# A weight-splitting kernel: the low part of every other weight unit on GpSimd instead of VectorE

## The chip, the cores and the metric

The kernel runs on 1 core of one Trainium2 chip. The metric is the device time in microseconds (us) of one execution. The program is written in Bass with its own semaphores: five engines (TensorE, VectorE, ScalarE, GpSimd, SyncE) each run a program of their own, and order between engines exists only where one waits for a count that another has raised. Inside an engine the program runs in the order in which it is written. The profile calls TensorE PE (its weight loads PEld), VectorE DVE, ScalarE ACT, GpSimd POOL and SyncE SP.

## The reference, cut to what matters

Two transformer blocks run one after the other on 256 tokens (272 in the first block, which puts 16 meta tokens ahead), each with two layers, width 1024, all in float32. Nearly all of the arithmetic is products with weight matrices:

```python
# first block, for each layer
h = h + mix                                   # layer 0: chunk scan + attention, layer 1: pooling
h = h + einsum('blf,fd->bld', relu(rmsnorm(h) @ w_mlp_up) ** 2, w_mlp_down)      # d_ff 4096
# second block, for each layer
x = x + rms_norm(mix, g)                      # layer 0: short convolution, layer 1: attention
gate, up = split(causal_dwconv(rms_norm(x) @ w_up, w_conv), 2)                   # 2 x 2816 columns
x = x + rms_norm((silu(gate) * up) @ w_down, g)
x = x + rms_norm(sigmoid(rms_norm(x) @ w_gate) * (p_i @ w_proj), g)
```

## The kernel before, in words

Activations lie with their features on the 128 partitions and the tokens along the free axis. Each product of float32 operands is made of three products of the shorter type fp32r: an operand v is split into a high part (v rounded to fp32r) and a low part (v minus the high part), and high x high, high x low and low x high are summed in PSUM (`products`, lines 333 to 342, the matmul is line 340; the variants `products_rows` and `first_products` have theirs on lines 351 and 385).

The weights are cut into 383 **units** of at most 128 x 1024 elements (`weight_units`, lines 19 to 84), numbered in the order in which TensorE uses them. 365 units are 1024 elements wide, 16 are 768 and 2 are 512. A unit passes through four steps:

- SyncE loads unit n into one of 4 buffers RAW (`load_unit`, line 309), after `wl` of unit n - 4, the sign that the low part of the unit that had the buffer is made.
- ScalarE copies it to fp32r into one of 7 buffers WH (`act_split`, line 318). It waits for the load and for `used` of unit n - 7.
- VectorE subtracts: WL = RAW - WH, into one of 7 buffers WL (`dve_split`, line 325), after `wh` of unit n.
- TensorE waits for `wl` of unit n and uses it in, mostly, 24 matmuls of 128 x 128 by 256 tokens.

The order of the steps is written out by hand. `act_split(a, upto)` and `dve_split(v, upto)` make all units below `upto` that are not yet made; the stages call them in between their own work, so that they run some 6 to 7 units ahead of TensorE. In the feed-forward stages of the second block (`vector_ffn`, lines 1859 to 1950) VectorE's loop runs over u = 0 to 24. Each of its steps covers two units of w_up: for m = 0 and 1 one split (of unit n0 + 2u + m + 6, n0 being the stage's first unit) and one FZ (line 1895, PSUM times the root's row RR); then two products YB (line 1877) or two low parts FL (line 1883); then four convolution taps (line 1457, on GB or YB). ScalarE makes the first tap from FZ (line 1826), the high part FH (line 1798) and its splits in the same order. n0 is unit 197 in the first of these stages (ffn0) and unit 307 in the second (ffn1); both are odd. The down product behind it (`tensor_output`, line 1461) reads FH and FL in blocks of 8, 8 and 6 chunks k and takes two units for each block.

A `Signals` object keeps for each event, such as ("wl", n), the semaphore and the count that stand for it. `mark` raises the semaphore of its kind, `also` makes one event stand for another, and a kind of semaphore may belong to one engine only. All programs are run through dry first, so that each wait knows its count.

GpSimd sets two constants (`gpsimd_start`, line 496) and clears five buffers of the first mixer (`gpsimd_mixer`, line 552). After that its program is over.

Of the kernel before, what the change touches and what calls it, by code (L numbers as in the profile page):

```python
# [12 lines left out]
NR = 4  # L13
NH = 7
# [72 lines left out]
def width(unit):  # L87
    return UW if unit[3] is None else len(unit[3]) * len(unit[4])
# [162 lines left out]
def program(nc, xin, pin, gains, cst, wpack, out):  # L251
    f32, f32r, u32 = mybir.dt.float32, mybir.dt.float32r, mybir.dt.uint32
    ALU, ACT, AX = mybir.AluOpType, mybir.ActivationFunctionType, mybir.AxisListType
    units = weight_units()
# [7 lines left out]
    NU = len(units)  # L262
    scratch = nc.dram_tensor("bias_rows", (8, 384), f32)
    ctx = ExitStack()
    with ctx:
        def sb(name, shape, dt=f32, scope=ctx):
            return scope.enter_context(nc.sbuf_tensor(name, shape, dt))

        sig = Signals(lambda kind: ctx.enter_context(nc.semaphore(f"s_{kind}")))
# [6 lines left out]
        RAW = [sb(f"RAW{i}", [128, UW]) for i in range(NR)]  # L276
        WH = [sb(f"WH{i}", [128, UW], f32r) for i in range(NH)]
        WL = [sb(f"WL{i}", [128, UW], f32r) for i in range(NH)]
# [32 lines left out]
        def act_split(a, upto):  # L311
            while a.units < min(NU, upto):
# [4 lines left out]
                    a.wait_ge("used", n - NH)  # L317
                a.e.activation(WH[n % NH][:, 0:w], RAW[n % NR][:, 0:w], ACT.Copy).then_inc(*a.mark("wh", n))  # L318

        def dve_split(v, upto):  # L320
            while v.units < min(NU, upto):
                n, v.units = v.units, v.units + 1
                w = width(units[n])
                v.wait_ge("wh", n)
                v.e.tensor_tensor(WL[n % NH][:, 0:w], RAW[n % NR][:, 0:w], WH[n % NH][:, 0:w].bitcast(f32),  # L325
                                  ALU.subtract).then_inc(*v.mark("wl", n))
# [169 lines left out]
        def gpsimd_start(p):  # L496
            p.e.memset(ONE[:, :], 1.0).then_inc(*p.mark("ones", 0))
            p.e.memset(EPS[:, :], 1e-6).then_inc(*p.mark("ones", 1))
# [53 lines left out]
        def gpsimd_mixer(p):  # L552
            for i, (z, val) in enumerate(((QB[:, :, :], 0.0), (KB[:, :, :], 0.0), (ATT[:, :, :], 0.0), (ATM[:, :, :], 0.0),
                                          (E[:, :, :], 1.0))):
                p.e.memset(z, val).then_inc(*p.mark("zero", i))
            p.wait_ge("zero", 4)
            p.e.memset(E[:, :, 0:1], 0.0).then_inc(*p.mark("zero", 5))
            p.wait_ge("zero", 5)
            p.e.memset(E[:, :, 16:T:64], 0.0).then_inc(*p.mark("zero", 6))
# [394 lines left out]
        def vector_mixer(v):  # L954
# [6 lines left out]
            def divided(key, uu, dst):  # L961
                for m in range(2):
                    h = 2 * uu + m
                    dve_split(v, unit_at[key, h] + NH - 1)
                    v.wait_ge("mix", key, h)
                    v.wait_ge("rk", "m")
                    v.e.tensor_tensor(dst[:, h, :], PS[:, banks.at[key, h], 0:T], R, ALU.mult).then_inc(
                        *v.mark("ev", key, h))
# [50 lines left out]
            def latent(x):  # L1019
                key = ("cq", "ckv")[x]  # L1020
                dve_split(v, unit_at[key, 0] + NH)
                for m in range(2):
                    o = CQ[:, 2 * x + m, :]
                    v.wait_ge("mix", key, m)
                    v.e.tensor_tensor(o, PS[:, banks.at[key, m], 0:T], R, ALU.mult).then_inc(*v.mark("ev", key, m))
                    v.wait_ge("ch", 2 * x + m)
                    v.e.scalar_tensor_tensor(out=CL[:, 2 * x + m, :], in0=o, scalar=g(("qa", "kva")[x], m),
                                             in1=CH[:, 2 * x + m, :].bitcast(f32), op0=ALU.mult,
                                             op1=ALU.subtract).then_inc(*v.mark("cl", 2 * x + m))
# [91 lines left out]
            v.e.tensor_tensor_scan(flat(B), flat(E), flat(LF), 0.0, ALU.mult, ALU.add).then_inc(*v.mark("scan"))  # L1121
            exponents(0)
            dve_split(v, unit_at["hi", 0] + NH)
            attention(0)
            prepare(0)
# [1192 lines left out]
        def gpsimd_program(p):  # L2318
            gpsimd_start(p)
            gpsimd_mixer(p)  # L2320

        def sync_program(s):
            sync_start(s)
            s.e.dma_start(C[:, :], cst[:, 128:NCA]).then_inc(*s.mark_dma("c"))
            for n in range(NR, NU):
                load_unit(s, n)
            for p in range(4):
                s.wait_ge("x2", "end", p)
                s.e.dma_start(out[:, 2 * p:2 * p + 2, :], X[:, 2 * p:2 * p + 2, NM:T]).then_inc(*s.mark_dma("out", p))
            s.wait_ge("out", 3)  # L2330
# [8 lines left out]
        for fill in (tensor_program, scalar_program, vector_program, gpsimd_program, sync_program):  # L2339
            counted(fill)  # L2340
# [16 lines left out]
        @block.gpsimd  # L2357
        def _(e):
            gpsimd_program(Engine("gpsimd", e, sig))
# [69 lines left out]
```

## Time and profile before

| | |
|---|---|
| Median of 3 runs | 1394.87 us (1394.56 to 1399.25) |
| The profiled execution's own time | 1391.52 us |
| Its span, first to last instruction | 1389.5 us |
| Mean granted clock of TensorE | 0.974 of 2.4 GHz |
| TensorE matmuls busy | 1330.0 us, 96% |
| VectorE busy | 918.8 us, 66% |
| ScalarE busy | 725.1 us, 52% |
| GpSimd busy | 4.5 us, 13 instructions |

The busy time of an engine is the time that at least one of its instructions covers. A row of a group gives busy time and the mean duration of one instruction; instructions of one engine overlap by a little in the records, so the distance between two starts is slightly below the duration. The chain that ended last is followed back from the last instruction, at each step to what released it.

### The profile page before, as it was taken

The page shows a single profiled execution, that of the slowest core. Times are in us where ns is not written, and L with a number is a line of the kernel's source. Part 1 is how long each engine was busy: PE and PEld are TensorE (multiplying, and loading weights), DVE is VectorE, ACT ScalarE, POOL GpSimd, SP SyncE. Part 2 cuts the span into 40 slices and gives each one's busy share as a digit, 9 for nine tenths or more (in the row PEclk, how much of TensorE's full clock was granted, in tenths as well). Part 3 has the DMA queues.
Part 4 walks back from the last instruction along what each step waited for, and adds up shares of the span by engine and source line. Part 5 has one row for each costly group of instructions (what it writes and reads, how often), then busy time and mean ns, then how long its engine had stood idle before and what let it go on. Part 6 is the DMA issues. An engine that isn't in the chain of part 4 may idle for free.

```text
span 1389.5 us, 25078 instructions
## 1 busy us (share of the span) xinstructions
PE 1330.0 (96%) x10558; PEld 1288.7 (93%) x10558; DVE 918.8 (66%) x1505; ACT 725.1 (52%) x1219; POOL 4.5 (0%) x13
## 2 busy tenths in 40 slices
PE   5998899999998999999999999999999999999996
PEld 5897679999998999999999999999987799999996
DVE  4687655765446777444875999746564546999654
ACT  5754234665332666334545666646453446666644
POOL 1000000000000000000000000000000000000000
PEclk9999979999999999999999999999898999999997
DMA  6232005555552465654753666663272133666630
GB/s 257 85 122 81 31 3 150 182 180 170 181 170 75 145 200 175 194 183 129 227 180 118 194 187 196 200 200 106 89 246 66 31 109 106 201 193 192 204 121 31
DMA packets 58415, 205.20 MB, mean 148 GB/s; under 512 B 6328, under 2 KB 8640, under 8 KB 58048
## 3 DMA queue, kind: packets, MB, share of 16 engines
q1 hardware_dynamic: 56816, 201.77, 46.0%
q10 hardware_dynamic: 1488, 1.85, 0.5%
q8 instruction: 83, 1.36, 0.4%
q14 instruction: 28, 0.23, 0.1%
HBM read 202.53 MB, written 1.06 MB: 147 GB/s over the span
## 4 chain that ended last, share of the span: by engine, by line
PE 85%; DVE 8%; ACT 5%; issue 1%; DMA 1%; ACTq 0%; DVEq 0%
PE PS L340 65%; PE PS L385 7%; PE PS L351 2%; PE PS L368 2%; PE PS L419 2%; PE PS L2020 1%; PE PS L2019 1%; ACT WH L318 1%; DVE WL L325 1%; PE PS L466 1%; PE PS L652 1%; DMA HB<-bias_rows 1%; DVE Z L1417 1%; PE PS L784 0%; PE PS L690 0%
## 5 line engine op out<-in xcount | busy, mean ns | idle before, releaser
L325 DVE TENSOR_TENSOR WL<-RAW,WH 128x1024 fp32r<-128x1024 f32 (+2 forms) x383 | 460.5, 1207 | 261.5 <-ACT WH L318 261.2
L318 ACT ACTIVATE WH<-RAW 128x1024 fp32r<-128x1024 f32 (+2 forms) x383 | 391.2, 1042 | 251.3 <-PE PS L340 222.0
L340 PE MATMUL PS<-UH,WH 128*128 128x256 f32 (+1 forms) x1624 | 462.9, 285 | 6.9 <-DVE UL L1402 3.0
L340 PE MATMUL PS<-UH,WL 128*128 128x256 f32 (+1 forms) x1624 | 462.6, 285 | 0.0
L340 PE MATMUL PS<-UL,WH 128*128 128x256 f32 (+1 forms) x1624 | 462.4, 285 | 0.0
L340 PEld LDWEIGHTS PS<-UH,WH 128*128 128x128 f32 x1624 | 309.1, 190 | 7.9 <-issue 4.7
L340 PEld LDWEIGHTS PS<-UH,WL 128*128 128x128 f32 x1624 | 309.1, 190 | 0.0
L340 PEld LDWEIGHTS PS<-UL,WH 128*128 128x128 f32 x1624 | 307.5, 189 | 0.0
L340 PE MATMUL PS<-HL,WH 128*128 128x272 f32 (+1 forms) x512 | 145.8, 285 | 0.0
L340 PE MATMUL PS<-HH,WH 128*128 128x272 f32 (+1 forms) x512 | 145.7, 284 | 0.0
L340 PE MATMUL PS<-HH,WL 128*128 128x272 f32 (+1 forms) x512 | 145.4, 284 | 0.0
L340 PE MATMUL PS<-FH,WH 128*128 128x256 f32 x352 | 98.6, 280 | 0.0
L340 PE MATMUL PS<-FL,WH 128*128 128x256 f32 x352 | 98.5, 280 | 0.0
L340 PE MATMUL PS<-FH,WL 128*128 128x256 f32 x352 | 98.5, 280 | 0.0
L340 PEld LDWEIGHTS PS<-HH,WL 128*128 128x128 f32 x512 | 96.6, 189 | 0.0
L340 PEld LDWEIGHTS PS<-HL,WH 128*128 128x128 f32 x512 | 96.3, 188 | 0.0
L340 PEld LDWEIGHTS PS<-HH,WH 128*128 128x128 f32 x512 | 96.1, 188 | 0.0
L385 PE MATMUL PS<-UH,WH 128*128 128x256 f32 (+1 forms) x256 | 73.9, 289 | 0.2
L385 PE MATMUL PS<-UL,WH 128*128 128x256 f32 (+1 forms) x256 | 72.0, 281 | 0.0
L385 PE MATMUL PS<-UH,WL 128*128 128x256 f32 (+1 forms) x256 | 72.0, 281 | 0.0
L340 PEld LDWEIGHTS PS<-FH,WH 128*128 128x128 f32 x352 | 66.2, 188 | 0.0
L340 PEld LDWEIGHTS PS<-FL,WH 128*128 128x128 f32 x352 | 66.2, 188 | 0.0
(346 smaller groups left out, 1976.9 us busy)
## 6 DMA issues: line engine op xcount, KB each, us to landing
RAW<-wpack SPq DMA_DIRECT2D x365, 512.0 KB, 3.6
RAW<-wpack SPq DMA_DIRECT2D x16, 384.0 KB, 3.5
X<-xin SPq DMA_DIRECT2D x1, 1088.0 KB, 5.1
C<-cst SPq DMA_DIRECT2D x1, 1072.0 KB, 10.0
HB<-bias_rows ACTq DMA_DIRECT2D x1, 1024.0 KB, 7.4
out<-X SPq DMA_DIRECT2D x4, 256.0 KB, 2.3
RAW<-wpack SPq DMA_DIRECT2D x2, 256.0 KB, 3.5
PI<-pin ACTq DMA_DIRECT2D x2, 256.0 KB, 3.1
```

The source lines that it names most:

```text
L318: a.e.activation(WH[n % NH][:, 0:w], RAW[n % NR][:, 0:w], ACT.Copy).then_inc(*a.mark("wh", n))
L325: v.e.tensor_tensor(WL[n % NH][:, 0:w], RAW[n % NR][:, 0:w], WH[n % NH][:, 0:w].bitcast(f32), ALU.subtract).then_inc(*v.mark("wl", n))
L340: ins = t.e.matmul(o, part(n, hw, kw, a, b), x(kx), start=first and not i and not p, stop=last and i == len(kcs) - 1 and p == 2)
L351: ins = t.e.matmul(o, x(kx), part(n, hw, kw, 0, w), start=not i and not p, stop=i == len(kcs) - 1 and p == 2)
L368: t.e.matmul(PS[:, b, 0:256], ONER[:, :], ONER[:, :].unsqueeze(1).to_broadcast([128, 2, 128]), start=True, stop=True)
L385: ins = t.e.matmul(PS[:, b, 0:w], part(n, hw, k, 0, 128), x_(k), start=k == 0 and p == 0, stop=k == 7 and p == 2)
L419: return t.e.matmul(o, src[:, m, a:z], ONE[:, 0:1], start=first and m == 0, stop=last and m == 1)
L466: ins = t.e.matmul(PS[:, b, a:z], rooted(st, x, n).to_broadcast([n, 128]), ID[0:n, 0:n], start=True, stop=True)
L652: ins = t.e.matmul(PS[:, b, 0:T], hot, x, start=n == 0 and hh == 0, stop=n == len(terms) - 1 and hh == 3)
L1417: v.e.tensor_tensor(Z[i][:, :, lo:T], src[:, :, lo:T], src[:, :, lo - k:T - k], ALU.add).then_inc(*v.mark("pz", gi, k))
L2019: t.e.matmul(o, c2("anti"), hb, start=True, stop=False)
L2020: ins = t.e.matmul(o, QH[ps_, h, q0:q0 + 128], KH[ps_, h, 0:w], start=False, stop=True)
```

## The change

GpSimd's program gets a third part. For n = 1, 3, 5, ... 381 it waits for `wh` of unit n and makes WL = RAW - WH with the same subtraction, marks an own semaphore `wlp`, and the event ("wl", n) now stands for it. `dve_split` skips the odd units. ScalarE, SyncE and TensorE are unchanged but for the semaphore on which ("wl", n) of an odd n is waited for.

```diff
+        def gpsimd_split(p):
+            for n in range(1, NU, 2):
+                w = width(units[n])
+                p.wait_ge("wh", n)
+                p.e.tensor_tensor(WL[n % NH][:, 0:w], RAW[n % NR][:, 0:w], WH[n % NH][:, 0:w].bitcast(f32),
+                                  ALU.subtract).then_inc(*p.mark("wlp", n))
+                sig.also(("wl", n), ("wlp", n))
+
         def dve_split(v, upto):
             while v.units < min(NU, upto):
                 n, v.units = v.units, v.units + 1
+                if n % 2:
+                    continue
                 w = width(units[n])
                 v.wait_ge("wh", n)
...
         def gpsimd_program(p):
             gpsimd_start(p)
             gpsimd_mixer(p)
+            gpsimd_split(p)
```

## Rows read from the trace of the kernel before

**Rows 1.** The page, part 1: busy time, share of the span, instructions.

```profile
span 1389.5 us, 25078 instructions
...
PE 1330.0 (96%) x10558; PEld 1288.7 (93%) x10558; DVE 918.8 (66%) x1505; ACT 725.1 (52%) x1219; POOL 4.5 (0%) x13
```

**Rows 2.** The chain that ended last: the page's shares by engine, then shares by line.

```profile
PE 85%; DVE 8%; ACT 5%; issue 1%; DMA 1%; ACTq 0%; DVEq 0%
...
by line: PE PS L340 65.5%; PE PS L385 6.8%; PE PS L351 2.1%; PE PS L368 1.7%; PE PS L419 1.5%; PE PS L2020 1.3%; issue 1.3%; PE PS L2019 1.2%; ACT WH L318 1.1%; DVE WL L325 1.1%; PE PS L466 0.9%; PE PS L652 0.6%; DMA HB<-bias_rows 0.5%; DVE
```

**Rows 3.** The page, part 5: the two groups that split the weights.

```profile
L325 DVE TENSOR_TENSOR WL<-RAW,WH 128x1024 fp32r<-128x1024 f32 (+2 forms) x383 | 460.5, 1207 | 261.5 <-ACT WH L318 261.2
L318 ACT ACTIVATE WH<-RAW 128x1024 fp32r<-128x1024 f32 (+2 forms) x383 | 391.2, 1042 | 251.3 <-PE PS L340 222.0
```

**Rows 4.** Waits of PE: line, releaser: us in total, times, longest us.

```profile
PE PS L419 <- DVE ACC L415: 14.5, 3, 10.2
...
PE PS L340 <- DVE WL L325: 2.7, 1, 2.7
```

**Rows 5.** Windows: busy us of PE, PEld, DVE, ACT, POOL; PEclk, DMA share, GB/s.

```profile
475.00:500.00 25.00, 25.00 (x214) 25.00 (x213) 20.67 (x33) 18.86 (x33) 0.00 (x0) 1.00 0.83 252
...
775.00:800.00 25.00, 25.00 (x214) 25.00 (x213) 24.65 (x48) 16.54 (x27) 0.00 (x0) 1.00 0.64 208
```

**Rows 6.** Timeline of DVE in ffn0: start us, us, line, operation, out<-in.

```profile
773.16 0.42 DVE L1895 TENSOR_TENSOR FZ<-PS,RR 128x256 f32<-128x256 f32 x1
...
777.91 0.42 DVE L1895 TENSOR_TENSOR FZ<-PS,RR 128x256 f32<-128x256 f32 x1
778.25 1.22 DVE L325 TENSOR_TENSOR WL<-RAW,WH 128x1024 fp32r<-128x1024 f32 x1
779.38 0.42 DVE L1895 TENSOR_TENSOR FZ<-PS,RR 128x256 f32<-128x256 f32 x1
779.72 0.75 DVE L1877 TENSOR_TENSOR YB<-YB,GB 128x256 f32<-128x256 f32 x2
...
788.78 0.42 DVE L1895 TENSOR_TENSOR FZ<-PS,RR 128x256 f32<-128x256 f32 x1
```

**Rows 7.** The chain in order of time, ffn0 and ffn1: start us, us, what.

```profile
759.14 2.82 PE PS L340 x24
...
762.40 170.60 PE PS L340 x1446
...
1169.02 170.60 PE PS L340 x1446
```

**Rows 8.** Timeline of PE where the down product of ffn0 begins.

```profile
873.01 0.28 PE L340 MATMUL PS<-FH,WH 128*128 128x256 f32 x1
```

**Rows 9.** Timeline of DVE at the end of ffn0's up stage.

```profile
876.58 0.42 DVE L1895 TENSOR_TENSOR FZ<-PS,RR 128x256 f32<-128x256 f32 x1
...
882.82 0.76 DVE L1883 SCALAR_TENSOR_TENSOR FL<-YB,FH 128x256 fp32r<-128x256 f32 x2
885.62 4.63 DVE L325 TENSOR_TENSOR WL<-RAW,WH 128x1024 fp32r<-128x1024 f32 x4 [2.04 <-ACT WH L318]
```

**Rows 10.** POOL: a group by line and form, and its last instruction in the timeline.

```profile
L555 POOL MEMSET ATT<- 128x1024 f32 x1 | 1.0, 951 | 0.0
...
4.98 0.12 POOL L559 MEMSET E<- 128x16 f32 x1
```

**Rows 11.** The page, part 6: DMA issues, KB each, us to landing.

```profile
RAW<-wpack SPq DMA_DIRECT2D x365, 512.0 KB, 3.6
```

**Rows 12.** Timeline of DVE in the first mixer: two operations of one size.

```profile
45.28 1.28 DVE L1105 SCALAR_TENSOR_TENSOR LF<-LF,B 128x1088 f32<-128x1088 f32 x1
...
47.81 0.73 DVE L1112 TENSOR_SCALAR B<-LF 128x1088 f32<-128x1088 f32 x1
```

**Rows 13.** Mixer, 93 to 125 us: the splits' group on DVE, and the chain there.

```profile
L325 DVE TENSOR_TENSOR WL<-RAW,WH 128x1024 fp32r<-128x1024 f32 x5 | 5.8, 1200 | 0.8 <-ACT WH L318 0.8
...
116.50 2.27 DVE WL L325 x2
```

## The prediction

> **What bounds the kernel now.** I read the busy shares first: TensorE is busy for 96% of the span, VectorE for 66%, GpSimd for nothing to speak of [rows 1]. The chain that ended last says the same: 85% of it are matmuls, 8% VectorE, 5% ScalarE, and the splits of line 325 hold only 1.1% of it, 15.3 us [rows 2]. The waits of TensorE agree: for a low part of a weight it waits once, 2.7 us; its longest wait for VectorE is for a sum of squares [rows 4]. So 460.5 us of splits on VectorE [rows 3] lie beside TensorE nearly everywhere, and an emptier VectorE gives little by itself. What counts is whether VectorE stays fast enough. The windows show where that is tight: in the MLP of the first block it is busy for 20.67 of 25 us at its fullest, but in the feed-forward stages of the second block for 24.65 of 25 us, with TensorE full and its granted clock at 1.00 [rows 5].
>
> How tight, the timelines tell. A pair of steps of the loop over u (4 units) takes VectorE 788.78 - 777.91 = 10.87 us, one step 5.43 [rows 6]. TensorE goes from 762.40, where unit (u=2, m=1) begins, to 873.01, where the down product begins, in 110.61 us for 39 units [rows 7, 8]: 2.836 us each, 5.67 for two. VectorE is thus 0.24 us a step faster, and needs it, as it starts late: unit (2,0) was done at 759.14 + 2.82 = 761.96 [rows 7], its FZ begins at 773.16 [rows 6], 11.2 us behind; the last FZ begins at 876.58 [rows 9], 3.6 us behind 873.01. The low parts FL of the last two chunks are made at 883.58 [rows 9]. TensorE wants them four units and four chunks after 873.01: 873.01 + 4 x 2.836 + 12 x 0.118 = 885.8, 2.2 us later. The next weight unit that VectorE splits (885.62 to 886.8 [rows 9]) is wanted at about 888.6 (four full units and two of 6/8 the length), 1.8 us later. So the stage can bear about **2 us** more of VectorE's time; beyond that TensorE waits one for one.
>
> **The change, part by part.**
> Removed: 191 of 383 splits on VectorE. A split takes it 779.38 - 778.25 = 1.13 us from start to start [rows 6], 216 us in all. All but the part on the chain (15.3 us, about half of it for odd units, 7.6) lies under TensorE and is worth nothing.
>
> Added on GpSimd: 191 subtractions with two inputs. The trace has none. The nearest rows: a memset of the same shape, which only writes, takes it 0.95 us [rows 10]. Reading two inputs and writing one result takes between one such pass (0.95) and three in turn (2.85). I take 2.3: two reads after one another, the write mostly beside them, some start cost. Cover: an odd unit comes every 5.67 us, so GpSimd keeps up up to there; and a unit is split 5 to 6 units (14 us) before its use, so 1.2 us more of latency is hidden. RAW is freed that much later too; SyncE's next load has some four units' time, 11 us, and lands after 3.6 [rows 11]. Nothing for both; without the cover it would be 1.2 us each time that TensorE stands and waits for an odd unit.
>
> Moved in order: GpSimd's program is empty behind 5.1 us [rows 10], so nothing is queued behind its waits. VectorE no longer stands before odd units for ScalarE (it stands 261.2 us for WH [rows 3], nearly all in stretches where it has nothing to do).
>
> Unknown: what VectorE and GpSimd do to each other in SBUF. In this trace they never read it together. Its bounds: nothing, or a VectorE instruction that reads two SBUF operands stands still as long as GpSimd reads. One pair of rows speaks for the latter: over 1088 elements a one-input operation from SBUF takes 0.73 us, a two-input one 1.28 [rows 12]. VectorE thus has two ways into SBUF and uses both for one input if it can; a two-input operation leaves no way free, and GpSimd must come in somewhere. Whether on a way of VectorE's, no row shows. I take the full block as likelier.
> The Trainium skill ("SBUF — State Buffer", Who interferes with whom) says that GpSimd's only read port is VectorE's second one and that whoever comes second with two SBUF inputs "fully blocks" until the first is done. By its "GPSIMD Engine Reference", Performance versus the Vector engine, a subtraction of 2048 elements takes 4497 ns, so some 2.25 us here (an estimate); the sum by this price would be about 2 us smaller.
>
> **The sum.** In a step of the loop the splits of m = 0 are odd units (n0 + 6 is odd in both stages) and go to GpSimd. All that is left on VectorE reads two SBUF operands, but for the two FZ, which read PSUM. GpSimd's 2.3 us stop it but for one FZ (779.72 - 779.38 = 0.34 us [rows 6]) that can run below them: 1.96 us. The step becomes 5.43 - 1.13 + 1.96 = 6.26 us, against TensorE's 5.67: VectorE becomes the bound of both stages. 21 steps with splits lengthen by 0.83 us each, 17.4 us; less the 2 us that the stage bears, 15.4. ffn1 has the same pace (170.60 us for 1446 matmuls in both [rows 7]): **+31 us** for the two. TensorE's stall falls on its wait for the bank that FZ frees, and on the splits of ScalarE, which stands behind FZ in its own order.
> With GpSimd's other ends: 0.95 us leaves a block of 0.61, shorter than the 1.13 removed, and costs 0; 2.85 gives 2.51 blocked, 29 - 2 = 27 a stage, +54.
> Elsewhere: the first MLPs have room (20.67 of 25 at their fullest). In the mixer, between 93 and 125 us, the chain runs over VectorE with five splits, 5.8 us [rows 13], of which three are odd (21, 23, 25): 3.4 us removed, up to 3 x 2.3 blocked, +3. At the other exits of stages the odd splits that leave the chain (7.6 - 3.4 = 4 us) and the blocks that enter it about cancel: 0. Together +34 on the profiled 1391.52 (span 1389.5 [rows 1] and 2 around it), 1426. The median stands 3.4 us above that execution; I predict **1428 us** as the median.
>
> **The rivals.**
> 1. *No interference* (faster side). GpSimd has its own way into SBUF. Then the odd splits simply leave the chain: at most 7.6 us, and some wait for WH behind them. Time 1395 - 8 = 1387, or less gain if ScalarE's WH takes their place. For it: no row shows a cost of sharing, though none had the occasion. Against it: the two operations of [rows 12]. It needs blocks near zero at the mixer and the gates; it decides if a block is under some 0.3 us.
> 2. *Interference that the stage can bear.* The engines take turns in small pieces or GpSimd's operation is short, and an operation costs VectorE between 0.3 and 1.2 us, less than the split removed. Point from which it decides: 1.13 + 2/21 = 1.23 us of block per GpSimd operation. Time 1390 to 1398. For it: VectorE's gaps at semaphores would let some of the reads through.
> 3. *GpSimd becomes the bound.* Were its operation above 5.67 us (because of the fp32r output, or because VectorE's unbroken row of operations lets it in late), TensorE waits for each odd unit: with 6.5 us, 0.8 x about 160 pairs, 130 us more. Nothing in the rows asks for it, the memset being 0.95 us.
> That GpSimd does not do its share in time is excluded: its program is free from 5 us on.
>
> **How the numbers follow.** Forecast (block longer than 1.23 us) 0.59, its own range 1405 to 1456; rival 1 0.22; rival 2 0.15; rival 3 0.04. This kernel's measurement can tell about 0.5%, 7 us. Rival 1 lies on both sides of that: 0.13 faster, 0.09 within. Rival 2 is within. So faster 0.13, same 0.24, slower 0.63. The range takes in rival 2, most of rival 1 and the 2.85 us end with 7 us for mixer and exits: 1386 to 1456; outside are rival 3, the best of rival 1 and a still slower GpSimd, under 0.2.
>
> **What would show it.** VectorE's group of line 325 with 192 instructions; on GpSimd a group of 191, near 2.3 us. In ffn0 and ffn1: the distance between FZ of the same m two steps apart 12.5 instead of 10.87 us, the two-input operations (the split at 1.22 us among them) with longer means or starts pushed apart, FZ from PSUM unchanged in length, matmul pieces of the chain broken by waits for FZ and for WH, and TensorE below 25 of 25 us in windows between 775 and 875. It would be wrong if the VectorE operations that overlap GpSimd's keep their lengths and spacing, or if the two stages last as before and the difference sits in the mixer or at the gates instead.

## The result, and the profile after

The changed kernel takes 1436.76 us (median of 4 runs, 1435.78 to 1437.77) against 1395.54 us beside it: a ratio of 1.029, 95% interval 1.0269 to 1.0312, 41 us slower. The forecast was 1428 us, 33 us slower than the 1394.87 us known then. In the profiled executions the span goes from 1389.5 to 1434.2 us.

The page of the changed kernel, parts 1, 4 and 5 (to be read beside [rows 1 to 3]; the new lines of the source push what was line 340 to 350, 325 to 335, 1457 to 1467):

```profile
span 1434.2 us, 25080 instructions
...
PE 1347.2 (94%) x10558; PEld 1299.1 (91%) x10558; DVE 860.5 (60%) x1314; ACT 724.8 (51%) x1219; POOL 481.8 (34%) x204
...
PE 67%; DVE 23%; ACT 6%; issue 3%; DMA 2%; POOL 0%; ACTq 0%; DVEq 0%
PE PS L350 48%; PE PS L395 7%; DVE GB L1467 5%; DVE YB L1467 5%; DVE WL L335 4%; PE PS L361 2%; ACT WH L318 2%; PE PS L378 2%; PE PS L429 1%; PE PS L2030 1%; PE PS L2029 1%; DVE FZ L1905 1%; DVE YB L1887 1%; DVE FL L1893 1%; PE PS L476 1%
...
L324 POOL TENSOR_TENSOR WL<-RAW,WH 128x1024 fp32r<-128x1024 f32 (+1 forms) x191 | 477.3, 2500 | 927.2 <-ACT WH L318 927.1
...
L335 DVE TENSOR_TENSOR WL<-RAW,WH 128x1024 fp32r<-128x1024 f32 (+2 forms) x192 | 291.6, 1520 | 277.0 <-ACT WH L318 277.0
```

Two things stand out. VectorE has lost 191 splits, 216 us of work, but its busy time falls by 58.3 us only (918.8 to 860.5): the others have become longer. The mean of its splits goes from 1207 to 1520 ns. And the chain that ended last, in which VectorE had 8%, now runs over VectorE for 23%, above all through the convolution taps of line 1467. GpSimd's subtraction takes 2.50 us on average (2.3 was taken). The groups of VectorE by form, in the changed kernel, show which operations grew:

```profile
L1467 DVE SCALAR_TENSOR_TENSOR GB<-FZ,G,GB 128x254 f32<-128x254 f32 x44 | 57.6, 1309 | 1.6
L1467 DVE SCALAR_TENSOR_TENSOR YB<-FZ,G,YB 128x254 f32<-128x254 f32 x44 | 53.5, 1215 | 1.6
L1905 DVE TENSOR_TENSOR FZ<-PS,RR 128x256 f32<-128x256 f32 x88 | 36.0, 411 | 8.1 <-ACT RR L484 8.1
...
L1343 DVE TENSOR_TENSOR HL<-TB,HH 128x256 fp32r<-128x256 f32 x32 | 23.1, 729 | 0.0
```

These are means: before, the taps of 254 elements took 483 ns on average, now 1309 and 1215. They mix taps that are stopped with taps that are not; one that is stopped takes 2.50 us (below), the others some 0.48 as before. FZ, whose product comes from PSUM, took 416 ns and takes 411. HL, the low part of the first block's MLP, reads two SBUF operands and went from 418 to 729 ns on average as well, under TensorE's cover. The timelines of the two engines in ffn0 put the blocks in their place (start us, us, engine, line, operation), first VectorE, then GpSimd, and last, from the chain, the fourth tap by itself:

```profile
803.56 0.41 DVE L1905 TENSOR_TENSOR FZ<-PS,RR 128x256 f32<-128x256 f32 x1
803.90 1.21 DVE L335 TENSOR_TENSOR WL<-RAW,WH 128x1024 fp32r<-128x1024 f32 x1
805.03 0.41 DVE L1905 TENSOR_TENSOR FZ<-PS,RR 128x256 f32<-128x256 f32 x1
805.36 0.74 DVE L1893 SCALAR_TENSOR_TENSOR FL<-YB,FH 128x256 fp32r<-128x256 f32 x2
806.03 3.92 DVE L1467 SCALAR_TENSOR_TENSOR YB<-FZ,G,YB 128x255 f32<-128x255 f32 x4
809.87 0.41 DVE L1905 TENSOR_TENSOR FZ<-PS,RR 128x256 f32<-128x256 f32 x1
810.21 1.21 DVE L335 TENSOR_TENSOR WL<-RAW,WH 128x1024 fp32r<-128x1024 f32 x1
```
```profile
800.69 2.67 POOL L324 TENSOR_TENSOR WL<-RAW,WH 128x1024 fp32r<-128x1024 f32 x1 [3.65 <-ACT WH L318]
807.01 2.66 POOL L324 TENSOR_TENSOR WL<-RAW,WH 128x1024 fp32r<-128x1024 f32 x1 [3.65 <-ACT WH L318]
```
```profile
807.45 2.50 DVE YB L1467
```

From the FZ at 803.56 to the one at 809.87 a step of the loop takes 6.31 us; it was 5.43 [rows 6], and 6.26 was forecast. ScalarE makes the high parts of the next two units while VectorE is in its four taps, and so GpSimd's subtraction, 2.66 us long in the records, falls on the taps. They took 1.91 us and take 3.92: the subtraction stops VectorE for **2.01 us**. Only the fourth tap is longer, 2.50 instead of 0.48 us. GpSimd's record begins 0.44 us before it, while the third tap is under way and is not stopped; these 0.44 us and another 0.2 us or so at the end make up the 0.65 us of the record that cost VectorE nothing.

So it goes in 17 of the 21 steps of ffn0. In the first three, GpSimd begins 0.90 us before VectorE's split, which was not ready yet and which it then stops for 1.45 to 1.47 us; an FZ runs in the meantime. The last of the 21, of a narrower unit, costs 1.59 us. This is one of the stopped splits; when nothing stops it, it takes 1.22 us:

```profile
777.94 2.69 DVE L335 TENSOR_TENSOR WL<-RAW,WH 128x1024 fp32r<-128x1024 f32 x1 [0.32 <-ACT WH L318]
```

Where the 44.7 us of span arise is seen from the starts of the first products (72 matmuls of line 385, now 395) in the chain in order of time. Before:

```profile
746.05 8.46 PE PS L385 x72
...
940.61 8.86 PE PS L385 x72
...
983.93 8.48 PE PS L385 x72
...
1152.64 8.48 PE PS L385 x72
...
1347.22 8.89 PE PS L385 x72
```

After:

```profile
750.48 8.48 PE PS L395 x72
...
963.48 8.88 PE PS L395 x72
...
1009.77 8.52 PE PS L395 x72
...
1179.04 8.48 PE PS L395 x72
...
1391.82 8.91 PE PS L395 x72
```

From its first product to that of the gate stage behind it, ffn0 goes from 940.61 - 746.05 = 194.56 to 213.00 us, **+18.4**, and ffn1 from 194.58 to 212.78, **+18.2**. The first gate stage with its exit goes from 43.3 to 46.3, +3.0. Before ffn0 the changed kernel is 4.4 us behind; all else changes by 0.6 us or less. So 36.6 of 44.7 us lie in the two feed-forward stages.

### The profile page after: what moved, and what is told of

The parts are those of the page before. It is cut to its first block, busy times and chain, and to the rows that moved or that the text cites. A ratio compares the mean times of both kernels' runs of the same rounds, so it can differ in the third digit from the quotient of the medians.

```text
span 1434.2 us, 25080 instructions
## 1 busy us (share of the span) xinstructions
PE 1347.2 (94%) x10558; PEld 1299.1 (91%) x10558; DVE 860.5 (60%) x1314; ACT 724.8 (51%) x1219; POOL 481.8 (34%) x204
## 4 chain that ended last, share of the span: by engine, by line
PE 67%; DVE 23%; ACT 6%; issue 3%; DMA 2%; POOL 0%; ACTq 0%; DVEq 0%
PE PS L350 48%; PE PS L395 7%; DVE GB L1467 5%; DVE YB L1467 5%; DVE WL L335 4%; PE PS L361 2%; ACT WH L318 2%; PE PS L378 2%; PE PS L429 1%; PE PS L2030 1%; PE PS L2029 1%; DVE FZ L1905 1%; DVE YB L1887 1%; DVE FL L1893 1%; PE PS L476 1%
## 5 line engine op out<-in xcount | busy, mean ns | idle before, releaser
L324 POOL TENSOR_TENSOR WL<-RAW,WH 128x1024 fp32r<-128x1024 f32 (+1 forms) x191 | 477.3, 2500 | 927.2 <-ACT WH L318 927.1
L350 PE MATMUL PS<-UH,WL 128*128 128x256 f32 (+1 forms) x1624 | 462.0, 284 | 0.0
L350 PE MATMUL PS<-UL,WH 128*128 128x256 f32 (+1 forms) x1624 | 461.8, 284 | 0.0
L335 DVE TENSOR_TENSOR WL<-RAW,WH 128x1024 fp32r<-128x1024 f32 (+2 forms) x192 | 291.6, 1520 | 277.0 <-ACT WH L318 277.0
L350 PE MATMUL PS<-FH,WH 128*128 128x256 f32 x352 | 102.3, 291 | 13.2 <-DVE FL L1893 11.3
L1467 DVE SCALAR_TENSOR_TENSOR GB<-FZ,G,GB 128x255 f32<-128x255 f32 x88 | 76.6, 892 | 1.6
L1467 DVE SCALAR_TENSOR_TENSOR YB<-FZ,G,YB 128x255 f32<-128x255 f32 x88 | 75.7, 881 | 1.6
```

The costliest lines, as they stand in the source:

```text
L324: p.e.tensor_tensor(WL[n % NH][:, 0:w], RAW[n % NR][:, 0:w], WH[n % NH][:, 0:w].bitcast(f32), ALU.subtract).then_inc(*p.mark("wlp", n))
L350: ins = t.e.matmul(o, part(n, hw, kw, a, b), x(kx), start=first and not i and not p, stop=last and i == len(kcs) - 1 and p == 2)
L1467: v.e.scalar_tensor_tensor(out=y[:, k:S], in0=src[:, 0:S - k], scalar=g(name, i0 + 2 - k), in1=y[:, k:S], op0=ALU.mult, op1=ALU.add).then_ ...
```

## The experiments

The expectations name the explanations by letters. Theory A is the prediction's: VectorE's operations with two SBUF inputs stand still while GpSimd reads SBUF. Rival S: handing units to a second engine costs by itself. Rival L: the odd units come too late. Rival W: GpSimd's writing blocks VectorE too. Theory C, later: part of the cost is TensorE's clock behind a stall.

The same measure of the two stages and of the first gate stage, taken from each kernel's chain, for all of them (us; "time" is the median, "before" that of the kernel before on the same chip):

| Kernel | time | before | ratio (95%) | ffn0 | ffn1 | gate 0 |
|---|---|---|---|---|---|---|
| before | | | | 194.56 | 194.58 | 43.3 |
| changed | 1436.8 | 1395.5 | 1.029 (1.0269 to 1.0312) | 213.0 | 212.8 | 46.3 |
| a1 narrow | 1391.5 | 1396.9 | 0.9961 (0.9946 to 0.9977) | 194.6 | 194.6 | 43.7 |
| a2 narrow, late | 1391.9 | 1396.9 | 0.9966 (0.9952 to 0.998) | 194.6 | 194.6 | 43.3 |
| a3 doubled | 1483.9 | 1396.9 | 1.0625 (1.0593 to 1.0657) | 236.1 | 237.5 | 43.4 |
| c1 memsets | 1395.0 | 1396.9 | 0.9989 (0.9966 to 1.0012) | 194.6 | 194.6 | 44.2 |
| a4 loops on VectorE | 1400.4 | 1396.0 | 1.003 (1.0012 to 1.0049) | 194.6 | 194.6 | 46.3 |
| b1 loops only | 1433.7 | 1396.0 | 1.0263 (1.0237 to 1.0289) | 211.8 | 212.3 | 43.3 |
| b2 quarter | 1417.2 | 1396.0 | 1.0146 (1.0123 to 1.0168) | 204.1 | 203.2 | 44.7 |
| c2 copy | 1426.4 | 1396.0 | 1.0204 (1.0181 to 1.0227) | 208.7 | 208.4 | 43.6 |
| d1 dummies | 1418.5 | 1399.0 | 1.0149 (1.0121 to 1.0177) | 203.2 | 204.7 | 44.8 |
| d2 away | 1397.0 | 1399.0 | 0.9995 (0.9984 to 1.0007) | 194.6 | 194.6 | 43.6 |
| e1 more dummies | 1422.6 | 1395.0 | 1.0178 (1.0132 to 1.0224) | 203.0 | 203.7 | 45.3 |

**Is it the reading, the lateness, or the handing over?**

Narrow: GpSimd subtracts only 64 columns of each odd unit, from unit 15 on.

```diff
                 w = width(units[n])
+                w = w if n < 14 else 64
                 p.wait_ge("wh", n)
```

> The changed kernel, but from unit 15 on GpSimd subtracts only the first 64 of the 1024 columns of an odd unit (the low parts of the other columns are left out, so the output is not the reference's). VectorE still makes only the even units. It shows what the change would be worth if GpSimd's operation cost next to nothing. Theory A (while GpSimd reads SBUF, VectorE's operations with two SBUF inputs stand still): the block shrinks from 2.0 us to about 0.2, a step of the feed-forward loop goes from 6.31 us back to TensorE's 5.67, and only what leaves the chain is left: 1384 to 1394 us. Rival L (the odd units come late, because GpSimd takes 2.5 us instead of 1.2): the same, as the narrow operation is early too. Rival S (splitting the order over two engines costs by its semaphores alone): about 1437 as in the changed kernel.

It took 1391.5 us, 0.4% less than before. The two stages are at 194.6 us again. With two semaphores, two engines and half of the splits gone from VectorE, but hardly any reading on GpSimd, nothing of the slowdown is left: rival S falls. It also tells about what the change could have brought: 5 us (3 to 8 by the interval). Its stages don't show where these 5 us come from; its profiled execution took 1392.85 us.

Narrow and late: the same, with three memsets ahead of the narrow subtraction in the two loops.

```diff
+                if in_ffn(n):
+                    for i in range(3):
+                        if ms:
+                            p.wait_ge("ms", ms[-1])
+                        ms.append(3 * n + i)
+                        p.e.memset(SPARE[n // 300][:, :], 0.0).then_inc(*p.mark("ms", 3 * n + i))
...
```

> As the narrow kernel, but in the two feed-forward stages GpSimd does three memsets of 128x1024 into a spare buffer (2.85 us, writes only) before each narrow subtraction, so that an odd unit is ready later than in the changed kernel without more reading. Theory A: within 3 us of the narrow kernel, the step of the loop stays at 5.67 us. Rival L (lateness): the two stages take 18 us each more than before, as in the changed kernel, so some 37 us above the narrow kernel. Rival W (GpSimd's writes block VectorE too): at least as much, a step of 5.43 - 1.13 + 2.85 = 7.1 us, some 60 us above.

1391.9 us, and 194.6 us a stage. Odd units that are ready more than 3 us after their high part cost nothing: rival L falls, and the cover that the prediction named for GpSimd's latency (units split 5 to 6 ahead) holds.

Doubled: the kernel before, and GpSimd repeats the odd subtractions of the loops into a spare buffer. VectorE still makes all low parts.

```diff
+            for n in range(1, NU, 2):
+                if in_ffn(n):
...
+                    p.e.tensor_tensor(SPARE[n // 300][:, 0:w], RAW[n % NR][:, 0:w], WH[n % NH][:, 0:w].bitcast(f32),
+                                      ALU.subtract).then_inc(*p.mark("dup", n))
...
```

> The kernel before, VectorE makes all low parts, and in the two feed-forward stages GpSimd makes those of the odd units once more, into a spare buffer that nobody reads; loads and high parts of a buffer wait until that is done. Theory A: each of the 21 doubled subtractions of a stage stops VectorE for 2.0 us, a step takes 5.43 + 2.0 = 7.4 us, a stage 21 x 2.0 - 2 = 40 us more, so about 1395 + 80 = 1475 us. Rival L: no unit that TensorE waits for is later, so 1395 to 1400.

1483.9 us, 87 us more, where nobody reads what GpSimd makes; only the loads and high parts wait until it has read their buffers. 1475 was expected: the 2 us that a stage was to bear aren't there. The stages grow by 41.6 and 43.0 us: 21 x 2.01 = 42.2. VectorE's step in its timeline, then GpSimd's:

```profile
803.47 0.41 DVE L1916 TENSOR_TENSOR FZ<-PS,RR 128x256 f32<-128x256 f32 x1
803.80 0.74 DVE L1898 TENSOR_TENSOR YB<-YB,GB 128x256 f32<-128x256 f32 x2
804.47 3.92 DVE L1477 SCALAR_TENSOR_TENSOR GB<-FZ,G,GB 128x255 f32<-128x255 f32 x4
808.32 1.21 DVE L345 TENSOR_TENSOR WL<-RAW,WH 128x1024 fp32r<-128x1024 f32 x1
```
```profile
805.45 2.66 POOL L337 TENSOR_TENSOR SPARE<-RAW,WH 128x1024 f32<-128x1024 f32 x1 [4.79 <-ACT WH L323]
```

The four taps take 3.92 us here too, at a GpSimd record of 2.66 us, and the step is 7.45 us, 2.02 more than 5.43; VectorE goes through these rows without a wait, so it is the block that lengthens the step and not the later buffers. The block is a property of the subtraction, not of the place of the low parts in the kernel.

Memsets: the kernel before, and three memsets at each odd unit of the loops.

```diff
+                    for i in range(3):
+                        if ms:
+                            p.wait_ge("ms", ms[-1])
+                        ms.append(3 * n + i)
+                        p.e.memset(SPARE[n // 300][:, :], 0.0).then_inc(*p.mark("ms", 3 * n + i))
```

> The kernel before, and in the two feed-forward stages GpSimd does three memsets of 128x1024 into a spare buffer at each odd unit: 2.85 us of writes, no reads. Theory A (it is the reading that blocks): 1395 us, no difference, VectorE's step stays 5.43 us. Rival W (any use of SBUF by GpSimd blocks): a step of 5.43 + 2.85 = 8.3 us, two stages of +58 us, about 1510.

1395.0 us, no difference that can be measured, and the rows show VectorE untouched while GpSimd writes for 3 us:

```profile
783.89 1.91 DVE L1473 SCALAR_TENSOR_TENSOR GB<-FZ,G,GB 128x255 f32<-128x255 f32 x4
785.72 1.22 DVE L341 TENSOR_TENSOR WL<-RAW,WH 128x1024 fp32r<-128x1024 f32 x1
```
```profile
784.86 2.99 POOL L334 MEMSET SPARE<- 128x1024 f32 x3 [1.78 <-ACT WH L319]
```

The taps take 1.91 us, as before. GpSimd's writing blocks nothing: rival W falls.

Copy: the kernel before, and GpSimd copies RAW of each odd unit of the loops to the spare buffer, one input instead of two.

```diff
+                    p.e.tensor_copy(SPARE[n // 300][:, 0:w], RAW[n % NR][:, 0:w]).then_inc(*p.mark("dup", n))
```

> The kernel before, and in the two feed-forward stages GpSimd copies RAW of each odd unit into a spare buffer: one input read instead of two. Theory A (any reading of SBUF by GpSimd blocks): a copy of 128x1024 should take about 1.1 us, block about as long, a step 5.43 + 1.1 = 6.5 us, a stage 21 x 1.1 - 2 = 21 us, so about 1438 us. If only two-input operations of GpSimd collide with VectorE: 1396 us.

1426.4 us; of the two outcomes that of "any reading blocks", but with a smaller size than expected:

```profile
804.20 2.56 DVE L1476 SCALAR_TENSOR_TENSOR YB<-FZ,G,YB 128x255 f32<-128x255 f32 x4
```
```profile
805.16 1.33 POOL L337 COPY SPARE<-RAW 128x1024 f32<-128x1024 f32 x1 [4.77 <-ACT WH L323]
```

The taps take 2.56 us, a block of 0.65 to 0.66 us at a record of 1.33; 21 x 0.66 = 13.9 us a stage, measured 14.1 and 13.8. I had expected a block of 1.1 us. Under the taps one input blocks for 0.65 us and two for 2.01, and in both cases the record is some 0.65 us longer than the block. That difference is not a property of GpSimd's operation: in the first three steps of ffn0 it begins only 0.15 to 0.19 us before the split that it stops, and there the block is 2.20 us at a record of 2.49 to 2.52 in the doubled kernel, 0.84 at 1.15 to 1.18 here. What escapes is above all the time until VectorE's next two-input instruction begins.

**Where does the cost lie, and how does it grow?**

> The changed kernel, but VectorE makes all low parts that are made inside the loops of the two feed-forward stages (units 8 to 49 from each stage's first); GpSimd has the odd units elsewhere. Theory A: both stages go back to TensorE's pace (37 of the changed kernel's 41 us gone), what stays is the mixer and the first gate stage: 1398 to 1406 us. If the cost were spread over all stages (rival S, semaphores and order), 149 of 191 odd units stay and with them some 32 us: about 1428.

```diff
+        pool_units = [n for n in range(1, NU, 2) if not in_ffn(n)]
...
-            for n in range(1, NU, 2):
+            for n in pool_units:
...
-                if n % 2:
+                if n in pool_units:
```

1400.4 us: 37 of 41 us are gone with 42 of 191 subtractions.

> The counterpart: GpSimd has the 42 odd units inside the two feed-forward loops and no others. Theory A: these 42 subtractions cost nearly all of it, 2 x 18 us: 1430 to 1435 us. Rival S: 42 of 191 of the cost, 9 us, 1405.

The edit is the same with `pool_units = [n for n in range(1, NU, 2) if in_ffn(n)]`. 1433.7 us, 38 us more than before. The two runs add up to the change, 4 + 38 against 41 us.

> The changed kernel with one unit in four (n = 1, 5, 9, ...) on GpSimd instead of one in two. Theory A: every second step of the loop is blocked, two steps take 5.43 + 6.31 = 11.74 us against TensorE's 11.34, so 10.5 x 0.40 - 2 = 2 us a stage, 4 for both, and half of what the mixer and the gate cost, 4: 1400 to 1407 us, a fifth of the cost for half of the work. A cost that goes by the number of units (rival S) gives half of it, 1417.

```diff
+        pool_units = [n for n in range(1, NU, 2) if n % 4 == 1]
```

A miss: 1417.2 us, by the number rival S's 1417 and not theory A's 1400 to 1407. The stages show that it isn't S (the rest of the kernel hardly grows): ffn0 takes 204.1 us, +9.5, and ffn1 203.2, +8.6. Two steps take 11.74 us, as expected, so VectorE is late by 10.5 x 0.88 = 9.2 us at the end of the loop. What failed in this expectation is the allowance: I had subtracted the 0.24 us a step by which VectorE is faster than TensorE, as if that reserve were free. It isn't: VectorE starts 11.2 us behind and arrives 3.6 us behind [rows 7 to 9], and it needs each of these steps to get there in time. Any lengthening of the loop arrives at its end in full. Of that the stage should have borne 2 us, and it bore nearly nothing.

> GpSimd has the odd units only where VectorE has time: not in the first mixer (units below 33), not in the two feed-forward loops, not around the first gate stage (265 to 280). Theory A: the blocks fall into VectorE's waits for WH, the time is that of the kernel before within 3 us, 1393 to 1398 us against 1396, perhaps 1 to 3 us less by the splits that leave the chain at the conv and attention stages. Rival S (a cost per unit handed over): some 120 units left of 191, 20 us more.

```diff
+        pool_units = [n for n in range(1, NU, 2) if 33 <= n and not in_ffn(n) and not 265 <= n < 281]
```

1397.0 us beside 1399.0, 0.9995 (0.9984 to 1.0007). For these 125 units together the change costs nothing and brings nothing, as the prediction had it for the MLPs. Whether a smaller choice among them would pay, no run shows.

**Why doesn't the stage bear its 2 us?** In the changed kernel TensorE's clock falls to half at the end of the loop (windows: busy us of PE, PEld, DVE, ACT, POOL, then the granted clock):

```profile
775.00:800.00 25.00, 25.00 (x214) 25.00 (x213) 24.08 (x37) 14.16 (x24) 10.37 (x4) 1.00 0.57 189
...
885.00:902.00 17.00, 12.61 (x104) 12.10 (x102) 16.79 (x29) 8.79 (x18) 4.98 (x3) 0.95 0.55 170
902.00:904.00 2.00, 1.65 (x6) 1.36 (x6) 1.93 (x6) 0.34 (x1) 0.00 (x0) 0.50 0.03 12
904.00:911.00 7.00, 5.31 (x26) 5.31 (x27) 3.87 (x6) 6.02 (x8) 2.95 (x2) 0.52 0.00 0
911.00:915.00 4.00, 4.00 (x36) 4.00 (x35) 3.85 (x2) 1.48 (x3) 3.38 (x2) 1.00 0.69 201
```

TensorE stands for 3.9 us, until 902.28, and for 1.8 us, until 905.69, before FL of the last chunks. The clock is already down when the first of these waits ends: between 902 and 911 us it is about 0.5, the lower level of 1.2 GHz; from 911 us on it is 1.00 again. Before the change the stretch from 885 to 925 us ran at 1.00 without a gap. What that costs, the chain tells:

```profile
905.21 0.44 DVE FL L1893
...
905.69 50.19 PE PS L350 x402
```

At the pace of [rows 7], 170.60 us for 1446 matmuls, 402 take 47.4 us; they take 2.8 us more here, and the only wait among them is the one at their start. So in the changed kernel the half clock alone takes what the stage should have borne. I tried to keep TensorE busy there, in the quarter kernel, which has the same stall.

```diff
...
                 for bi, (k0, kn) in enumerate(blocks):
+                    if (gg, bi) == (0, 2):
+                        keep_going(t, 28)
```

> The quarter kernel (1417 us), and in both feed-forward stages TensorE does 28 matmuls of ones with ones (3.3 us, their result unused) before the third block of the down product, where it would stand still for 3.6 us waiting for the last FL and then go on at half clock for some 60 matmuls. Theory C (VectorE's delay beyond the stage's 2 us is all that idle time costs by itself, and the rest of the 9 us a stage is the clock that fell behind the stall): the clock stays high, some 4 us a stage come back, 1409 to 1412 us. If the clock is no part of the cost: 1417 us, or more if the dummies get in the way.

1418.5 us, no gain. The 28 dummies filled the first gap only; a second of 2.6 us before the last two chunks stayed, and some half clock behind it (0.92 on average from 890 to 912 us, where the quarter kernel had 0.74 from 884 to 904).

```diff
...
+                        ks = [(k, k0 + k) for k in range(kn)]
+                        if (gg, bi, m) == (0, 2, 0):
+                            keep_going(t, 28)
+                            products(t, PS[:, bs[m], 0:S], n, ks[:4], 0, 128, hh, hl, ready, False, False)
+                            keep_going(t, 22)
+                            ks = ks[4:]
...
```

> The quarter kernel with idle time filled at both places: 28 dummy matmuls before the third block of the down product and 22 (2.6 us) before its last two chunks, where the kernel with 28 alone still stood for 2.6 us and fell to half clock afterwards. Theory C (a stall of a few us costs TensorE its clock behind it): no stretch at half clock is left at the end of the two stages, a stage takes 200 to 201 us instead of the quarter kernel's 204.1 and 203.2, together 1410 to 1412 us. If the clock is no part of the cost: 1417 us or more.

Now the clock stays up in the profile of this kernel (first fence; the quarter kernel in the second), but the stages take 203.0 and 203.7 us instead of 204.1 and 203.2: nothing that adds up to a gain, and the time, 1422.6 us with an interval of the ratio up to 1.0224, isn't lower.

```profile
896.00:904.00 8.00, 7.40 (x60) 6.98 (x58) 5.71 (x14) 5.06 (x9) 0.00 (x0) 1.00 0.06 23
```
```profile
895.00:903.00 8.00, 6.24 (x29) 5.95 (x29) 5.27 (x11) 6.02 (x8) 0.99 (x1) 0.50 0.08 16
```

The chain of this kernel tells why (start us, us, what):

```profile
900.21 1.28 ACT L493
...
901.61 1.05 ACT WH L318
...
902.69 1.24 DVE WL L340
...
904.06 45.10 PE PS L355 x378
```

Behind VectorE's and ScalarE's last work of the loop stand a table load of 1.28 us, the next high part and the next low part, and TensorE goes on only at 904.06. A faster clock merely brings it earlier to a unit that isn't split yet. Theory C's gain doesn't show in the time: in this profile the time that the clock gives back is mostly spent in front of the next wait.

## Why the prediction was right or wrong

Right in sign, in place and in mechanism. By its steps:

- *Unknown: full block or nothing.* Full block, as far as GpSimd reads: shown by the doubled kernel (cost though nobody reads its result), the memsets (no reading, no cost) and the narrow kernels. The rule in the Trainium skill ("SBUF — State Buffer", Who interferes with whom), that a VectorE instruction with two SBUF inputs contends with a GpSimd instruction that reads SBUF, not with one that only writes, and that the one that issues second is blocked, agrees with these rows: 0.48 to 2.50 us for the tap that comes second, 416 to 411 ns for FZ.
- *GpSimd's price.* 2.3 us were taken; the record is 2.40 where VectorE has nothing to stop, 2.50 on average and 2.66 beside the taps. (The row of the Trainium skill's "GPSIMD Engine Reference", Performance versus the Vector engine, from which the prediction's estimate of 2.25 us comes is that of an addition; it is 0.15 below the 2.40.) The block, 1.96 forecast and 2.01 measured, came out right by luck, two errors against each other: the price was 0.36 us too low, and the 0.34 us that I took off, for an FZ that would run under the subtraction, 0.31 us too little. From the fourth step on no FZ does run there; ScalarE's order puts the subtraction under the taps, and what doesn't block are 0.65 us, mostly the tap that is under way when it begins.
- *The step.* 6.26 forecast, 6.31 measured. The bound of 1.23 us per block from which it costs holds the 2 us that the stage was to bear; without them it is the 1.13 us of the split that goes, and no run has a block between the two. One sign that was named fails: TensorE is still full from 775 to 800 us. Where it stands later, it is before low parts of odd units (28 of the 29 short waits below lie in the two loops) and before FL, and not, as forecast, for the bank that FZ frees.
- *The sum of the stages.* 2 x 15.4 = 31 forecast, 18.4 + 18.2 = 37 measured. This is the term that was mis-sized. The 21 steps alone give 21 x 0.88 = 18.5; the 2 us that the stage was to bear weren't there. In all kernels with a block the stage grows by about what VectorE's loop grows: from the first product of ffn0 to VectorE's last pair of FL it is 14.3 us more in the copy kernel, 9.4 in the quarter kernel, 18.0 in the changed and 42.6 in the doubled one, and the stages grow by 14.1, 9.5, 18.4 and 41.6. (For the changed kernel: 905.21 - 750.48 = 154.7 against 882.82 - 746.05 = 136.8 us [rows 9].) In the changed kernel the half clock takes 2.8 us where 2.2 were to be gained: 18.0 - 2.2 + 2.8 = 18.6, and 18.4 was measured. With the clock kept up, the row of table load, high part and low part behind the loop came next; how much would then be left, the last two runs don't settle, and this stays open.
- *Elsewhere.* For the exits I had set gains against blocks, 0. The first gate stage costs 3.0 us, in the changed kernel and in a4: its product MM (line 1930), two SBUF inputs, on the chain between ScalarE's sigmoid and square, meets GpSimd three times. Before it took 0.69 us on average, now:

```profile
983.73 1.61 DVE L1930 TENSOR_TENSOR MM<-MM,TMA 128x512 f32<-128x512 f32 x1 [1.19 <-ACT TMA L1852]
...
989.40 1.53 DVE L1930 TENSOR_TENSOR MM<-MM,TMA 128x512 f32<-128x512 f32 x1 [2.26 <-ACT TMA L1852]
...
994.98 1.55 DVE L1930 TENSOR_TENSOR MM<-MM,TMA 128x512 f32<-128x512 f32 x1 [0.86 <-ACT TMA L1852]
```

  That is 0.92 + 0.84 + 0.86 = 2.6 us of the 3.0; the same stage takes 43.3 to 44.2 us in kernels where GpSimd has nothing to do in it. The mixer's +3 isn't shown: ffn0's first product starts at 750.5 us in the changed kernel, 4.4 later than before, but also at 750.6 in b1, where GpSimd has nothing of the mixer, and at 745.1 to 749.5 in the narrow, doubled, copy, memset and away kernels; this start varies by itself.
- *Rivals.* No interference: the narrow kernel shows what it would have given, 5 us, where 8 was put as the most. Bearable interference: the block of 2.01 us lies above its 0.3 to 1.2. GpSimd as the bound: TensorE has 29 short waits for its low parts, 11.1 us in all, in the row below, but the chain that ended last has 0% of GpSimd, its operation is far below 5.67 us, and in the doubled kernel, where TensorE waits for none of its work, the block is the same.

```profile
PE PS L350 <- DVE FL L1893: 11.3, 4, 3.9
PE PS L350 <- POOL WL L324: 11.1, 29, 0.5
```

## What to carry to other kernels

A second engine that relieves VectorE is no relief while it reads SBUF: count its reading time as VectorE's (here 2.01 of 2.66 us) wherever VectorE's operations have two SBUF inputs, and move work only if the block is shorter than what it takes away (here 1.13 us). Look for the stage where the helped engine is nearly full, not at its mean of 66%: 42 of 191 moved operations made nine tenths of the loss. And an engine that is faster than the bound while it makes up for a late start has no reserve; compare when it must arrive, not its pace.

## What the runs showed that I had not expected

- The second input of GpSimd's operation costs VectorE more than the first: a block of 0.65 us for one input and 2.01 for two under the taps, 0.84 and 2.20 where it begins just before a split. A VectorE instruction that is already under way is not stopped.
- The block stands in the profile as one longer VectorE instruction (2.50 us instead of 0.48), not as idle time; VectorE's busy share hides it.
- GpSimd can write 3 us beside VectorE's two-input operations without changing a row of theirs by more than 0.01 us.
- Around two stalls of TensorE of 3.9 and 1.8 us its granted clock was at half for some 9 us (902 to 911), in a stretch where it had been full before; filling the stall with dummies kept the clock at 1.00, and gained nothing, as the next wait was close.
